# Hybrid RWKV-7 / sparse-attention step on one core: value products and turned pieces of the prompt attention in groups of four

## The chip, the cores and the metric

One Trainium2 chip, one of its cores. The time is that of the device in microseconds (us) for one execution of the whole kernel; several runs are shown, and the median is compared. The hardware profile is of one execution.

## What is computed

One layer of a hybrid decoder for a prompt of 1024 tokens and for 8 sampled tokens. After a projection, the kernel computes a recurrent branch (RWKV-7) and an attention branch with three parts: over compressed keys (63 of them), over selected blocks (for the prompt all earlier ones, since there are no more than 16 blocks of 64), and over a window of 512. Only the prompt's attention matters here. For each of 8 query tiles of 128 tokens, 8 heads in 2 groups, and 3 branches:

```python
s_s = jnp.einsum('btgjd,btgnld->btgjnl', qg, k_g) - slopes * s_dist
p_s = masked_softmax(s_s, s_dist >= 0)
o_s = jnp.einsum('btgjm,btgmd->btgjd', p_s, v_g)
...
o = g[:, :, 0] * o_c + g[:, :, 1] * o_s + g[:, :, 2] * o_w
```

All is float32. The sums of the three branches are added up in one place, since the gates and the reciprocal row sums are multiplied into the probabilities before the value products.

## The kernel before

The prompt attention is `attend_prompt` (L1759), one stage of the kernel between barriers. Its work is cut into 32 units n (4 heads of each group, j = n // 8, by 8 query tiles in the order 0, 4, 7, 1, 6, 2, 5, 3). The two groups g of a unit go together, as two matmuls for each block of keys. A unit goes through these steps:

- S, scores (L1817, TensorE): a step is up to 512 key columns, two groups, into PSUM banks 0 to 3; steps alternate between two bank pairs, and a step waits until the masks of the step two before are done. There are 88 steps.
- masks (L1911, VectorE): adds the distance term, writes the scores to SBUF and takes their extreme.
- exponentials (L1870, ScalarE), with row sums. They are held back and issued at the next even score step, for the two steps before it.
- row sums to reciprocals (L1919, L1921, VectorE), then the scaling with gates (L1965, GpSimd), 6 instructions for a unit.
- T, turned pieces (L1830, TensorE): a piece is two key blocks of 128, transposed for both groups, that is 4 transposes, into one PSUM bank: bank 4 for even pieces, bank 5 for odd ones. Before it, TensorE waits for the scaling and for the copy of the piece two before, which frees the bank.
- copies of turned pieces to SBUF (`probsT`, 5 slots): even pieces by ScalarE (L1886), odd ones by VectorE (L1942). A copy waits for its piece and for the value products that free its slot.
- V, value products (L1844, TensorE): for a piece 4 matmuls, recorded as 8 instructions, accumulated in bank 6 or 7 by the parity of the unit. Before them TensorE waits for the piece's copy, and at a unit's first piece for the closing product of the unit two before.
- closing product (L1927, VectorE), once per unit, after its last value products.

`PromptPlan` (L1636) writes the order out by hand, as one list of events that TensorE, ScalarE and VectorE all walk; each takes its own part of an event (VectorE does masks at S, odd copies at T, the closing product at V). GpSimd goes through the units by itself, SyncE only issues stores and weights. For every two score steps, `turns` adds the pieces: the value products of the pieces that were turned in the round before (`waiting`), and the next up to four turned pieces (`now`, five if more than 8 queue up). So a round is S S, then the pieces. At the end of the stage, rounds marked R have no scores. There are 160 pieces. Full rounds read S S V V T T V V T T; some have fewer of one or the other. `turns` stands at L1701 to L1708.

Of the kernel before, what the change touches and what calls it, by code (L numbers as in the profile page):

```python
# [1635 lines left out]
class PromptPlan:  # L1636
# [64 lines left out]
    def turns(self, s, queue, waiting, ready):  # L1701
        while ready < self.N and self.last_step[ready] + AT_LEAD <= s:
            queue = queue + list(range(self.first_of[ready], self.last_piece[ready] + 1))
            ready += 1
        now = queue[:AT_GROUP + (len(queue) > 8)]
        for a in range(0, max(len(waiting), len(now)), 2):
            self.events += [("V", pc) for pc in waiting[a:a + 2]] + [("T", pc) for pc in now[a:a + 2]]
        return queue[len(now):], now, ready  # L1708

    def by_need(self, n):  # L1710
# [1921 lines left out]
```

## Time and profile before

| | us |
|---|---|
| median of 3 runs | 1786.95 |
| lowest and highest | 1781.71, 1788.53 |
| profiled execution, its own time | 1775.88 |
| its span (first to last instruction) | 1774.1 |
| prompt attention in it | 754.1 to 999.2 |
| its three passes of the same shape | 59.50, 59.86, 59.49 |
| TensorE busy in the span | 1690.9 (95%) |
| VectorE, ScalarE, GpSimd busy | 814.6, 577.2, 376.7 |
| mean granted TensorE clock | 0.983 of full speed |

The profile names engines PE (TensorE matmul), PEld (TensorE weight load, which overlaps PE), DVE (VectorE), ACT (ScalarE), POOL (GpSimd) and SP (SyncE). In a timeline a row is several like instructions in a row, with the start, the time from the first start to the last end, and in brackets the idle time of the engine before it and who ended it. "issue" is idle time for which the profile shows no wait. Weight loads show the rhythm of TensorE best, since the ends of matmuls are modelled. A turned piece has 4 weight loads, a value piece 8.

### The profile page before, as it was taken

The numbers are of one execution on the slowest core, as the hardware profiler recorded it, in microseconds if no ns is written. First come the engines' busy times: TensorE is split into PE (matmuls) and PEld (weight loads), VectorE is DVE, ScalarE is ACT, GpSimd is POOL, SyncE is SP. The second block draws the span as 40 slices with busy tenths as digits, with TensorE's granted clock in tenths as the row PEclk, the third lists the DMA queues.
The fourth block names the chain that finished last, engine by engine and source line by source line (L and its number), as shares of the span: only waits on it lengthen the run. The fifth ranks groups of instructions, "written<-read, shape, count | busy, mean of one in ns | idle before, by whom it ended". The sixth has DMA issues, their size and how long they took to land. (4 is left out here: it accounts for less than half of the span.)

```text
span 1774.1 us, 40928 instructions
## 1 busy us (share of the span) xinstructions
PE 1690.9 (95%) x17848; PEld 1157.7 (65%) x17848; DVE 814.6 (46%) x1684; ACT 577.2 (33%) x1229; POOL 376.7 (21%) x442
## 2 busy tenths in 40 slices
PE   7999889999999989999999899899999999899997
PEld 5666566666666645667666689776568888545443
DVE  3100165455545419077666666272133356633444
ACT  4111245344343211276666221113322221111444
POOL 0211233232212100055655322103300013100110
PEclk9999899999999999999999899899999999999999
DMA  4112001000100045091200497529720141510001
GB/s 159 48 36 54 2 3 27 14 15 15 26 15 15 15 125 74 1 251 49 96 2 1 125 306 285 173 77 214 189 52 24 48 142 25 220 42 1 24 24 48
DMA packets 115463, 135.88 MB, mean 77 GB/s; under 512 B 48252, under 2 KB 97093, under 8 KB 110334
## 3 DMA queue, kind: packets, MB, share of 16 engines
q1 hardware_dynamic: 106034, 83.97, 17.2%
q0 software_dynamic: 9216, 49.29, 9.0%
q8 instruction: 142, 2.33, 0.6%
q14 instruction: 35, 0.29, 0.1%
q10 hardware_dynamic: 36, 0.01, 0.0%
HBM read 120.64 MB, written 16.62 MB: 77 GB/s over the span
## 5 line engine op out<-in xcount | busy, mean ns | idle before, releaser
L845 PE MATMUL ps<-xnT,rw_side_w 128*128 128x344 f32 x576 | 204.0, 479 | 0.0
L566 PE MATMUL ps<-xnT,w_z 128*128 128x344 f32 x624 | 182.0, 453 | 2.3 <-DVE xnT L654 1.3
L566 PEld LDWEIGHTS ps<-xnT,w_z 128*128 128x128 f32 x624 | 117.9, 190 | 62.9 <-issue 1.5
L1965 POOL TENSOR_SCALAR probs<-probs,row_sums,gates 128x63 f32<-128x63 f32 (+6 forms) x148 | 95.6, 662 | 229.8 <-DVE row_sums L1921 229.3
L845 PEld LDWEIGHTS ps<-xnT,rw_side_w 128*128 128x128 f32 x576 | 99.2, 191 | 40.3 <-issue 3.3
L2232 PE MATMUL ps<-xnT,zT 128*128 128x344 f32 x384 | 120.8, 463 | 0.0
L2232 PEld LDWEIGHTS ps<-xnT,zT 128*128 128x128 f32 x384 | 71.7, 194 | 36.0 <-issue 5.6
L278 PE MATMUL ps<-w_kv,xnT 128*128 128x396 f32 x256 | 89.6, 509 | 3.5 <-DMA w_kv<-in_w_in_dram 3.4
L1870 ACT ACTIVATE probs<-probs,neg_max 128x63 f32<-128x63 f32 (+6 forms) x148 | 87.5, 595 | 1.5 <-DVE neg_max L1911 1.5
L1817 PE MATMUL ps<-kT,zT 64*128 64x512 f32 (+3 forms) x384 | 73.7, 496 | 2.6 <-PEq L82 1.4
L278 PEld LDWEIGHTS ps<-w_kv,xnT 128*128 128x128 f32 x256 | 48.8, 194 | 40.7 <-DMA w_kv<-in_w_in_dram 7.8
L1844 PE MATMUL ps<-probsT,kvtok 128*64 128x128 f32 x1056 | 75.3, 280 | 0.0
L682 DVE SCALAR_TENSOR_TENSOR zT<-z_diff,vec,zT 128x1032 f32<-128x1032 f32 x13 | 16.8, 1294 | 126.2 <-POOL z_diff L540 113.5
L1830 PE MATMUL ps<-ident,probs 128*128 128x128 f32 (+1 forms) x460 | 68.1, 280 | 5.1 <-DVE probsT L1942 3.4
L1886 ACT ACTIVATE probsT<-ps 128x512 f32<-128x512 f32 (+1 forms) x80 | 45.9, 574 | 82.6 <-PE ps L1830 82.6
L1844 PEld LDWEIGHTS ps<-probsT,kvtok 128*64 128x64 f32 x1056 | 56.0, 136 | 24.0 <-issue 23.0
L2936 POOL TENSOR_TENSOR mT<-mT,gate_n 128x258 f32<-128x258 f32 x28 | 23.7, 854 | 218.0 <-DVE gate_n L2899 218.0
L1344 POOL TENSOR_TENSOR rw_Lb<-rw_Lm,level_mask 128x512 f32<-128x512 f32 x40 | 53.9, 1355 | 63.8 <-DVE rw_Lm L1513 38.8
L1942 DVE COPY probsT<-ps 128x512 f32<-128x512 f32 (+1 forms) x80 | 50.5, 632 | 36.0 <-PE ps L1830 35.1
L2835 ACT ACTIVATE zT<-ps 128x258 f32<-128x258 f32 x72 | 27.8, 387 | 109.0 <-PE ps L2819 86.2
L1830 PEld LDWEIGHTS ps<-ident,probs 128*128 128x128 f32 (+1 forms) x460 | 49.8, 140 | 17.9 <-issue 10.5
L628 ACT ACTIVATE zT<-ps 128x344 f32<-128x344 f32 x39 | 17.3, 464 | 132.7 <-PE ps L566 132.7
(560 smaller groups left out, 3263.7 us busy)
## 6 DMA issues: line engine op xcount, KB each, us to landing
w_z<-in_w_in_dram SPq DMA_DIRECT2D x13, 512.0 KB, 3.8
xnT_kept<-xnT SPq DMA_DIRECT2D x1, 4128.0 KB
x_tok<-in_x_prompt_dram SPq DMA_DIRECT2D x8, 512.0 KB
rw_side_w<-in_w_in_dram SPq DMA_DIRECT2D x16, 256.0 KB, 3.3
zT<-in_w_in_dram SPq DMA_DIRECT2D x8, 512.0 KB, 5.3
ring_k<-in_w_in_dram SPq DMA_DIRECT2D x8, 512.0 KB, 5.3
w_out<-in_w_out_dram SPq DMA_DIRECT2D x1, 4096.0 KB
h_tok<-in_x_prompt_dram SPq DMA_DIRECT2D x8, 512.0 KB, 8.4
```

The costliest lines, as they stand in the source:

```text
L278: last = nc.tensor.matmul(k.ps[:, u % 4, 0:half], k.xnT[:, c, i * P:(i + 1) * P], w[:, c, h * half:(h + 1) * half], start=(c == 0), stop=( ...
L566: last = nc.tensor.matmul(k.ps[:, u % 6, 0:CG], w[:, n % w_ring, c, :], k.xnT[:, c, g * CG:(g + 1) * CG], start=(c == 0), stop=(c == KC - 1))
L845: ins = nc.tensor.matmul(k.ps[:, SIDE_BANKS[g % 2], 0:CG], w.side[:, t % 2, c, :], k.xnT[:, c, g % 3 * CG:(g % 3 + 1) * CG], start=(c == 0 ...
L1344: nc.gpsimd.tensor_tensor(w.Lb[:, n % 2], w.Lm[:].rearrange("p q c n -> p (q c) n"), bc(k.tab["level_mask"][:, n + 1, :], 1, 8), ALU.mult) ...
L1817: last = nc.tensor.matmul(k.ps[:, 2 * (s % 2) + g, at:at + w], k.qT[half(g), j, i * P:(i + 1) * P], keys[half(g), t0:t0 + w], start=True, ...
L1830: last = nc.tensor.transpose(k.ps[0:m, 4 + pc % 2, (2 * b + g) * P:(2 * b + g + 1) * P], region(n, br, g, t * P, m), k.ident[:])
L1844: last = nc.tensor.matmul(k.ps[half(g), 6 + n % 2, 0:P], vals, pt[0:m, pc % NPT, (2 * b + g) * P:(2 * b + g + 1) * P], start=(br == 1 and ...
L1870: nc.scalar.activation(every, every, ACT.Exp, scale=-1.0, bias=neg_m[:, at:at + 1], accum_out=ls[:, at:at + 1]).then_inc(expd, 1)
L1886: nc.scalar.activation(to, src, ACT.Copy).then_inc(pt_a, 1)
L1942: nc.vector.tensor_copy(to, src).then_inc(pt_v, 1)
L1965: nc.gpsimd.tensor_scalar(every, every, ls[:, at:at + 1], k.gates[:, i, gate:gate + 1], ALU.mult, ALU.mult).then_inc(scaled, 1)
L2232: ins = self.nc.tensor.matmul(self.k.ps[:, self.banks[n % nb], 0:CG], self.w[:, t % 2, c, :], self.k.xnT[:, c, g * CG:(g + 1) * CG], start ...
```

## The change

In each round all value products come first, then all turned pieces, where before they came two and two in turn. Nothing else in the list changes, neither which pieces a round has nor where the exponentials stand. A full round reads S S V V V V T T T T.

```diff
--- before.py
+++ after.py
@@ -1703,8 +1703,7 @@
             queue = queue + list(range(self.first_of[ready], self.last_piece[ready] + 1))
             ready += 1
         now = queue[:AT_GROUP + (len(queue) > 8)]
-        for a in range(0, max(len(waiting), len(now)), 2):
-            self.events += [("V", pc) for pc in waiting[a:a + 2]] + [("T", pc) for pc in now[a:a + 2]]
+        self.events += [("V", pc) for pc in waiting] + [("T", pc) for pc in now]
         return queue[len(now):], now, ready
```

## Rows read from the trace of the kernel before

**Rows 1.** The page, busy time of each engine.
```profile
PE 1690.9 (95%) x17848; PEld 1157.7 (65%) x17848; DVE 814.6 (46%) x1684; ACT 577.2 (33%) x1229; POOL 376.7 (21%) x442
```

**Rows 2.** Stretches, two passes: length, busy us (instructions) by engine, clock, DMA.
```profile
780.84:840.34 59.50, 58.09 (x574) 41.06 (x572) 41.78 (x175) 39.53 (x116) 31.01 (x49) 1.00 0.29 104
840.34:900.20 59.86, 58.09 (x574) 41.06 (x572) 41.69 (x175) 39.51 (x116) 34.96 (x52) 1.00 0.19 72
```

**Rows 3.** Waits in the prompt attention: total us, times, longest.
```profile
ACT probsT L1886 <- PE ps L1830: 82.6, 70, 3.2
...
PEld ps L1844 <- issue: 27.9, 93, 0.8
...
PEld ps L1830 <- POOL probs L1965: 11.7, 26, 1.5
...
PE ps L1830 <- DVE probsT L1942: 5.1, 12, 1.3
```

**Rows 4.** Timeline, weight loads of one full round: start, us, engine, instructions.
```profile
780.84 0.85 PEld L1844 LDWEIGHTS ps<-probsT,kvtok 128*64 128x64 f32 x16 [0.76 <-issue]
781.86 0.86 PEld L1830 LDWEIGHTS ps<-ident,probs 128*128 128x128 f32 x8 [0.17 <-issue]
782.89 0.85 PEld L1844 LDWEIGHTS ps<-probsT,kvtok 128*64 128x64 f32 x16 [0.17 <-issue]
783.91 0.41 PEld L1830 LDWEIGHTS ps<-ident,probs 128*128 128x128 f32 x4 [0.17 <-issue]
...
784.94 0.30 PEld L1817 LDWEIGHTS ps<-kT,zT 64*128 64x128 f32 x4 [0.17 <-issue]
```

**Rows 5.** Timeline of the same round, copies of turned pieces.
```profile
782.56 0.60 ACT L1886 ACTIVATE probsT<-ps 128x512 f32<-128x512 f32 x1 [3.17 <-PE ps L1830]
783.00 0.69 DVE L1942 COPY probsT<-ps 128x512 f32<-128x512 f32 x1
```

**Rows 6.** Timeline, weight loads of the last rounds.
```profile
997.24 1.29 PEld L1844 LDWEIGHTS ps<-probsT,kvtok 128*64 128x64 f32 x24 [0.17 <-issue]
```

**Rows 7.** Timeline of a round with two value and four turned pieces.
```profile
776.03 0.86 PEld L1830 LDWEIGHTS ps<-ident,probs 128*128 128x128 f32 x8 [0.17 <-issue]
...
776.73 0.60 ACT L1886 ACTIVATE probsT<-ps 128x512 f32<-128x512 f32 x1 [0.80 <-PE ps L1830]
...
777.44 0.42 PEld L1830 LDWEIGHTS ps<-ident,probs 128*128 128x128 f32 x4 [0.55 <-POOL probs L1965]
...
777.54 0.68 DVE L1942 COPY probsT<-ps 128x512 f32<-128x512 f32 x1
...
778.34 0.42 PEld L1830 LDWEIGHTS ps<-ident,probs 128*128 128x128 f32 x4 [0.47 <-POOL probs L1965]
```

**Rows 8.** Stretches, rounds, each to the next scores; columns as in rows 2.
```profile
776.04:778.92 2.88, 2.27 (x18) 1.69 (x16) 2.15 (x14) 1.38 (x4) 2.88 (x6) 1.00 1.23 159
...
786.65:789.80 3.15, 3.15 (x40) 2.30 (x38) 2.56 (x14) 3.15 (x9) 0.40 (x1) 1.00 0.63 205
797.47:801.34 3.87, 3.87 (x48) 3.19 (x47) 2.61 (x9) 1.34 (x5) 0.10 (x1) 1.00 0.48 204
802.56:805.92 3.36, 3.36 (x40) 2.51 (x38) 2.74 (x12) 2.34 (x7) 1.68 (x2) 1.00 0.43 180
807.41:811.24 3.83, 3.48 (x38) 2.76 (x37) 3.18 (x25) 1.68 (x7) 2.91 (x6) 1.00 0.01 1
813.15:817.67 4.52, 4.14 (x50) 3.41 (x48) 3.35 (x12) 2.25 (x11) 2.81 (x7) 1.00 0.01 4
819.59:823.73 4.14, 4.06 (x48) 3.17 (x46) 3.37 (x11) 2.63 (x7) 1.58 (x2) 1.00 0.00 0
```

**Rows 9.** Stretches at the end of the stage, columns as in rows 2.
```profile
984.78:990.58 5.80, 4.10 (x41) 3.18 (x41) 1.85 (x5) 3.53 (x11) 5.45 (x9) 1.00 0.00 0
990.58:995.16 4.58, 4.58 (x57) 3.90 (x58) 1.76 (x3) 1.19 (x2) 1.12 (x3) 1.00 0.00 0
995.16:999.02 3.86, 3.86 (x54) 2.88 (x50) 1.03 (x3) 0.60 (x1) 0.00 (x0) 1.00 0.02 4
```

## The prediction, made before the change was run

> **What bounds the kernel now.** I read the page first, then the stretch that the change touches, then single rounds of it. The page says that TensorE is busy for 95% of the span [rows 1]. The prompt attention runs from 754.1 to 999.2 us (the table ahead), and in a whole pass of it TensorE is busy for 58.09 of 59.50 us at a granted clock of 1.00 [rows 2], which is its upper level of 2.4 GHz. So the order of its own work decides, and every wait that is put into its queue is paid in full unless one beside it goes. The waits say what the other engines do there: ScalarE, before its copies of turned pieces, sat idle 82.6 us for TensorE; TensorE waited for VectorE's copies only 5.1 us in 12 places [rows 3]. The copiers have time to spare, but a sum says nothing on how fast one copy answers.
>
> One round then shows the pattern [rows 4]: weight loads of two value pieces (16 loads, 0.85 us), a gap of 0.17, two turned pieces (0.86), a gap of 0.17, again two and two, and the next scores. The gap stands at each change of kind, whatever the semaphores do: the profile calls it "issue". The copies of the same round [rows 5] begin 0.70 us after the first turned piece's load (781.86 to 782.56, ScalarE, 0.60 long) and 1.14 us after it for the second piece (783.00, VectorE, 0.69 long). There are two PSUM banks for turned pieces, so the third piece waits for the first one's copy, the fourth for the second one's. In this round the third is loaded at 783.91, 0.75 us after the first copy ended at 783.16: the two value pieces between cover that answer entirely.
>
> **What the change does, step by step.** It permutes the events of a round; TensorE, ScalarE and VectorE all walk the same list, so nothing is added or removed, no DMA moves, and SyncE's and GpSimd's queues don't read the list. By the plan in the code 45 rounds have pieces (160 pieces in all), in four passes over the same eight query tiles, one for each pair of heads; I take a pass from one full round to the next like it, 59.50 us [rows 2].
>
> Step 1, what it saves. Changes of kind between value and turned pieces go from 117 to 48 in the list. Three value pieces in a row are there at the end of the stage: 24 loads in 1.29 us and no gap inside [rows 6]. So four take 1.72 + 0.17 = 1.89 us where two pairs take 2 x 1.02 = 2.04. Two changes fewer in a full round are worth 0.30 us, if nothing waits.
>
> Step 2, what it costs. The four turned pieces now stand together, with nothing between the second and the third. This too is in the trace, in the round of two value and four turned pieces that both orders share [rows 7]: loads at 776.03, ScalarE's copy from 776.73 for 0.60, the third piece at 777.44, that is 1.41 us after the first, 0.11 behind the end of the copy. (The row names GpSimd as releaser of this gap; the ScalarE copy ends at 777.33, just ahead of the load, and I take it for the releaser.) Without the wait it would follow at about 0.86 + 0.06. The second piece's copy is VectorE's: 1.14 + 0.69 + 0.12 = 1.95 us after the first load the fourth can start, and 0.58 later come the scores (778.34 to 778.92, the end of the first stretch of rows 8). So the block takes 1.95 + 0.58 = 2.53 us, where two pairs take 2 x 1.03 = 2.06. If VectorE has the first piece of the block, the third starts at 0.70 + 0.69 + 0.11 = 1.50, the fourth at 1.97, and the block takes 2.55.
>
> A full clean round is then 1.89 + 2.53 = 4.42 us after its scores, against 4.10 now [rows 4, 8]: 0.32 more. In the shared round of rows 7 the fourth piece came later still (2.31), because VectorE was at its masks and row sums when the second piece was ready. In the new order the turned pieces start a microsecond later behind the scores and VectorE is through: in rows 5 it comes to its copy straight from other work, 2.16 us after the first value piece (780.84 to 783.00), and the new order wants it there at 1.89 + 1.14 = 3.03. So I take 1.95, not 2.31; the 2.31 is the upper bound.
>
> Step 3, the other rounds of a pass, by the same pitches [rows 8]. In order of time, now and then: 4.10 to 4.42; 3.15 to 3.02 (only two turned pieces, a change of kind saved, no wait); the shared round stays; 3.87 to 4.41 (a small third piece covers less); 3.36 to 3.75; 3.83 to 4.15; 4.52 to 4.55; 4.14 to 4.48; and three more of these shapes, read in the same view, +0.37, +0.26 and +0.35. The 4.52 round gains almost nothing in length because it already has the wait (TensorE is busy for 4.14 of it): VectorE's copy came late behind masks, and in the new order it ends at the same moment. In the 3.83 round the closing product of a tile (L1927, 0.28 us), which VectorE now does before its copy and not behind it, adds 0.2 to a copy that TensorE waits for. The sum is +2.8 us per pass (0.32 - 0.13 + 0 + 0.54 + 0.39 + 0.32 + 0.03 + 0.34 + 0.98). The pattern stands three times; in the second pass, which is 59.86 us long, the extra 0.36 is such a late copy in the 4.14 round, which then adds nothing. So 3 x 2.79 - 0.34 = 8.0; the next four rounds, of the first four kinds, give 0.7, one round near the start -0.1.
>
> Step 4, the end of the stage, where there are no scores and five turned pieces may stand in a row [rows 9]. The last round with scores is of the 3.36 kind; what follows it starts 0.36 later. In the next stretch of 5.80 us TensorE is busy for only 4.10: it waits for copies that stand behind row sums and exponentials; the exponentials stand behind a copy that is 0.36 later, and VectorE's copy gets the product of 0.28 in front of it: +0.3. Then 4.58 to 4.84, and the last stretch, whose last value pieces wait for the last turned pieces' copies without two value pieces as cover, 3.86 to 4.29. Together 0.36 + 0.3 + 0.26 + 0.43 = +1.3 us.
>
> The other queues: score steps wait for the masks of two steps before. By rows 5 VectorE is through with the masks 2.16 us into a round and the next scores come 4.10 us into it, so a longer round only gives more room. GpSimd's scaling is waited for in 26 places, 11.7 us together [rows 3]; most of them are the 0.17 gap under another name, and pieces that start later wait less: between -2 and 0, I take 0. The value pieces' own wait is on copies of the round before, which end while the next scores run. Behind the stage comes a barrier, and the next stage starts with it: nothing catches the delay up.
>
> The sum: 8.0 + 0.7 - 0.1 + 1.3 = **+9.9 us**. The profiled execution took 1775.88 us, 1.8 more than its span of 1774.1 and 11 less than the median of 1786.95 (the table ahead); the same steps stand in either, so I add the same 9.9: 1785.8 for an execution like the profiled one, 1796.9 for the median.
>
> One rule on the clock bears on this. In the shared round four turned pieces took 2.88 us and the granted clock was 1.00 throughout [rows 8], the upper level; TensorE was busy for 2.27 of it. The Trainium skill, page "TensorE: Matmul & The Clock Gate", section "Part 4: PE-mode transpose", says that transposes do not count as activity for the clock in the way matmuls do, which speaks against grouping them. By it the fourth rival below would hold; the trace's own group of four does not agree.
>
> **The rivals.** First, the other side: the third piece doesn't wait. If a copy answered within the 0.92 us that two turned pieces last, only step 1 would be left, some 69 changes of kind at 0.15 = -10 us: 1777. The point is 1.41 us against 0.92, and rows 7 measure 1.41; the ScalarE copy alone is 0.60. Chance 0.03.
>
> Second, the wait is hidden in most rounds as in the 4.52 one: if VectorE's and ScalarE's copies come late already, the old order pays the same. Then only some rounds add, half of the sum: +4 to +6, 1792. For it speak the 5.1 us that TensorE waits for VectorE now [rows 3]; against it, that TensorE is idle in few rounds (none in 3.87 of 3.87 and 3.36 of 3.36 [rows 8]). Chance 0.17.
>
> Third, the block is as long as in rows 7, 2.89 us and not 2.53, because a copier is late there too: 0.36 more in about 25 rounds, +9: +19, 1806. Against it stands the later start behind masks. Chance 0.13.
>
> Fourth, the clock falls to its lower level of 1.2 GHz in the groups: their 1.7 us of loads and more double in some 40 rounds, +70 us, 1865. Rows 8 speak against it. Chance 0.01.
>
> My forecast has 0.66, with an own range of 1793 to 1801: between the bounds of the waits (about 2 us either way) and the spread of medians.
>
> **How the numbers follow.** The likeliest case gives 1796.9. The runs shown spread from 1781.71 to 1788.53, so a median of a few moves by 2 to 3 us. The range reaches down into the second rival and up to the edge of the third: 1789 to 1805. About 0.5%, or 8.9 us, is what a measurement of this kernel can tell from no change, and +9.9 lies just over it. Of the forecast's 0.66 I give 0.40 to slower by over 0.5% and 0.26 to within; the third and fourth give 0.14 to slower, the second 0.02 to slower and 0.15 to within, the first 0.03 to faster. That is slower 0.56, within 0.41, faster 0.03.
>
> **What would show it.** In the profile after, a full round should have 32 value loads in one row of 1.7 us, one gap of 0.17, 8 loads of turned pieces, then an idle of about 0.5 us put down to ScalarE's or VectorE's copy, and some 4.4 us to the next scores; TensorE's wait for ScalarE's copies, hardly there now, should come near 10 us, and "issue" at the value pieces from 27.9 us down by some 5 to 7. TensorE's busy time should hardly change. If the third piece comes under 1.2 us after the first, step 2 is wrong; if the fourth comes at 2.3, the third rival holds; if the stage grows by under 7 us with these waits seen, the pitches of step 1 are too small; if anything behind 999.2 us moves other than by the shift, the carry through the barrier is wrong.

## The result and the profile after

The changed kernel is slower: 1793.45 us (20 runs, 1782.84 to 1801.44) against 1780.68 (20 runs, 1771.2 to 1788.53), a ratio of 1.0069 with a 95% interval of 1.0048 to 1.0091. In a second comparison on another occasion (the first experiment below) the ratio was 1.0029, 0.9997 to 1.0062. One of the ten runs of after in it took 1985.83 us at a granted clock of 0.841, where the others had 0.981 to 0.984, and is left out of the ratio. Both intervals hold what the traces of the attention say: it grew by 10.0 us, 0.56% of the whole. The median of before over more runs is 6 us lower than that of the first three, on which the forecast's absolute time was built.

| us | before | after |
|---|---|---|
| profiled execution, its own time | 1775.88 | 1797.99 |
| span | 1774.1 | 1796.1 |
| prompt attention, first score matmul to last value matmul | 244.74 | 254.76 |
| the rest of the span | 1529.4 | 1541.3 |
| TensorE busy in the span | 1690.9 | 1694.9 |
| granted clock | 0.983 | 0.981 |

The profiled execution of after is 22 us longer, and 12 of these lie outside the attention; a section below says what they are. All lines of the changed function stand one lower in the profile of after (L1829 for L1830).

A clean round is one in which TensorE waits for nobody in before. The full clean round that [rows 4] and [rows 5] show for before, in the timeline of after (start, us, engine, instructions, idle before and its end):

```profile
782.73 1.73 PEld L1843 LDWEIGHTS ps<-probsT,kvtok 128*64 128x64 f32 x32 [0.76 <-issue]
784.63 0.85 PEld L1829 LDWEIGHTS ps<-ident,probs 128*128 128x128 f32 x8 [0.17 <-issue]
785.32 0.60 ACT L1885 ACTIVATE probsT<-ps 128x512 f32<-128x512 f32 x1 [4.08 <-PE ps L1829]
785.76 0.69 DVE L1941 COPY probsT<-ps 128x512 f32<-128x512 f32 x1 [0.99 <-PE ps L1829]
786.03 0.41 PEld L1829 LDWEIGHTS ps<-ident,probs 128*128 128x128 f32 x4 [0.55 <-issue]
786.06 0.63 PE L1829 MATMUL ps<-ident,probs 128*128 128x128 f32 x4 [0.34 <-ACT probsT L1885]
786.56 0.42 PEld L1829 LDWEIGHTS ps<-ident,kT 128*128 128x128 f32 x4
...
787.15 0.30 PEld L1816 LDWEIGHTS ps<-kT,zT 64*128 64x128 f32 x4 [0.17 <-issue]
```

Four value pieces in one row of 32 loads, 1.73 us, and one gap of 0.17: 1.90 from the first of them to the first turned piece. The third turned piece comes 1.40 us after the first (784.63 to 786.03), 0.11 behind the end of ScalarE's copy; the row of the weight loads calls this idle time "issue", the matmul row of the same moment names the copy. The fourth comes 1.93 after the first, 0.11 behind VectorE's copy. The scores follow at 4.42.

Stretches of after: the three passes [rows 2], then rounds of the first, in order, that answer to [rows 4] and [rows 8] (length, busy us and instructions of PE, PEld, DVE, ACT, POOL, granted clock, DMA):

```profile
782.74:845.09 62.35, 58.12 (x576) 41.08 (x574) 42.15 (x175) 39.75 (x116) 30.98 (x49) 1.00 0.28 102
845.09:907.69 62.60, 58.11 (x576) 41.07 (x574) 42.39 (x174) 39.74 (x116) 34.94 (x52) 1.00 0.18 69
907.69:969.99 62.30, 58.13 (x576) 41.10 (x574) 42.19 (x175) 39.74 (x116) 30.90 (x48) 1.00 0.01 2
...
782.73:787.15 4.42, 4.08 (x50) 3.41 (x48) 2.73 (x9) 1.02 (x2) 0.09 (x1) 1.00 1.12 337
788.87:791.87 3.00, 3.00 (x41) 2.31 (x39) 2.23 (x13) 2.23 (x7) 0.35 (x1) 1.00 0.61 203
799.60:804.02 4.42, 3.95 (x50) 3.19 (x48) 2.58 (x7) 1.62 (x5) 0.08 (x1) 1.00 0.56 238
805.24:808.99 3.75, 3.41 (x42) 2.51 (x40) 2.69 (x12) 2.12 (x7) 2.09 (x3) 1.00 0.67 283
810.47:814.48 4.01, 3.48 (x40) 2.76 (x38) 3.16 (x25) 1.66 (x7) 2.70 (x6) 1.00 0.00 1
816.40:820.92 4.52, 3.98 (x52) 3.43 (x50) 3.35 (x11) 2.23 (x11) 2.60 (x7) 1.00 0.02 4
822.84:827.46 4.62, 4.18 (x50) 3.14 (x48) 3.53 (x11) 2.61 (x7) 2.08 (x3) 1.00 0.00 0
```

Passes are 2.85, 2.74 and 2.81 us longer than the 59.50, 59.86 and 59.49 of before, TensorE's busy time in them is the same (58.12 against 58.09), and the clock is at its upper level. The waits, against [rows 3] (total us, times, longest):

```profile
PEld ps L1843 <- issue: 24.4, 72, 0.8
...
PEld ps L1829 <- issue: 20.2, 68, 1.0
PEld ps L1829 <- POOL probs L1964: 11.7, 22, 0.9
PEld ps L1829 <- POOL kT L1964: 6.1, 8, 1.6
PE ps L1829 <- DVE probsT L1941: 5.6, 14, 0.8
...
PE ps L1829 <- ACT probsT L1885: 4.9, 14, 0.5
```

The same two kinds of row in before, which [rows 3] does not show:

```profile
PEld ps L1830 <- issue: 13.2, 62, 0.7
...
PE ps L1830 <- ACT probsT L1886: 0.3, 1, 0.3
```

TensorE waits for ScalarE's copies 14 times, where before it did once (0.3 us). This view alone would mislead: the same wait stands here under "issue", under ScalarE and, where a scaling came about as late, under GpSimd. The rounds' lengths are what adds up.

### The profile page after: what moved, and what is told of

Its sections match the earlier page's. It is cut to its first block and busy times, and to the rows that moved or that the text cites. A ratio compares the mean times of both kernels' runs of the same rounds, so it can differ in the third digit from the quotient of the medians.

```text
span 1796.1 us, 40928 instructions
## 1 busy us (share of the span) xinstructions
PE 1694.9 (94%) x17848; PEld 1159.7 (65%) x17848; DVE 814.8 (45%) x1684; ACT 578.0 (32%) x1229; POOL 376.7 (21%) x442
## 5 line engine op out<-in xcount | busy, mean ns | idle before, releaser
L1829 PE MATMUL ps<-ident,probs 128*128 128x128 f32 (+1 forms) x460 | 69.4, 279 | 14.1 <-ACT probsT L1885 4.6
L1843 PE MATMUL ps<-probsT,kvtok 128*64 128x128 f32 x1056 | 70.9, 278 | 0.5 <-ACT probsT L1885 0.5
L1829 PEld LDWEIGHTS ps<-ident,probs 128*128 128x128 f32 (+1 forms) x460 | 49.6, 140 | 29.3 <-issue 17.2
```

The lines of the kernel that those rows point to most:

```text
L1829: last = nc.tensor.transpose(k.ps[0:m, 4 + pc % 2, (2 * b + g) * P:(2 * b + g + 1) * P], region(n, br, g, t * P, m), k.ident[:])
L1843: last = nc.tensor.matmul(k.ps[half(g), 6 + n % 2, 0:P], vals, pt[0:m, pc % NPT, (2 * b + g) * P:(2 * b + g + 1) * P], start=(br == 1 and ...
```

## The experiments

All lengths of "the attention" run from the first score matmul to the last value matmul, 244.74 in before and 254.76 in after. Three comparisons below rest on 10 or more runs of each kernel and give a ratio (the changed kernel again, and the two orders with turned pieces on both sides); every other experiment is one profiled execution, and only its trace is read.

**The changed kernel again.** No edit.

> The changed kernel once more, unchanged. Theory (the order of the attention alone costs time, what lies behind it only shifts): the prompt attention is again 10.0 us longer than the 245.1 us of before, to 0.3 us, and the 8 to 9 us that TensorE waits in the compression of the sampled caches in the first profile of after (at its first use of the value weights cmp_w1v) come and go from one execution to the next, in the kernel before as well. Rival (the later start makes these weights collide with the gathers): the wait of 8 to 9 us is there again, and it belongs to the change.

```profile
756.08:1011.40 255.32, 235.48 (x2287) 165.88 (x2288) 168.70 (x687) 160.27 (x465) 127.06 (x196) 0.99 0.23 70
```

The attention took 255.3 us, 10.6 more than before: a little over the 0.3 us I had allowed. The stretch from the first score matmul to the first turned piece, which is the same in both orders, is where the two profiles of after differ (before, after, after again):

```profile
754.13:763.27 9.14, 7.88 (x40) 4.23 (x40) 6.62 (x37) 7.62 (x25) 2.37 (x6) 0.74 0.96 403
...
756.58:765.15 8.57, 7.41 (x40) 4.04 (x40) 6.62 (x37) 7.62 (x25) 2.36 (x6) 0.79 1.01 426
...
756.08:765.27 9.19, 8.49 (x40) 4.37 (x40) 6.62 (x37) 7.62 (x25) 2.36 (x6) 0.68 0.96 401
```

Its 40 matmuls take 8.57 to 9.19 us, the shorter the higher the granted clock (0.79, 0.74, 0.68 of full speed). From the first turned piece on, the attention took 235.60 us in before, 246.19 in after and 246.13 in after again: the change costs 10.6 and 10.5, and the 10.0 of the first profile holds 0.6 us of a faster start. The wait in the compression stage was not there; the 12 us outside the attention in the first profile of after shrink to 3 (1787.7 - 255.3 = 1532.4). The ratio here is 1.0029 (0.9997 to 1.0062).

**Copies slowed in both orders.** Ahead of each copy of a turned piece its engine copies 256 columns to a place that nobody reads (the diff is cut: a semaphore wait of each engine on its own earlier extra copy and the two buffers are left out here):

```diff
+                    nc.scalar.activation(aside[0][0:m, :], src[:, 0:256], ACT.Copy).then_inc(twice_a, 1)
                     nc.scalar.activation(to, src, ACT.Copy).then_inc(pt_a, 1)
...
+                    nc.vector.tensor_copy(aside[1][0:m, :], src[:, 0:256]).then_inc(twice_v, 1)
                     nc.vector.tensor_copy(to, src).then_inc(pt_v, 1)
```

In the order of before:

> The order of before, but ahead of each copy of a turned piece its engine copies 256 columns of it to a place that nobody reads, 0.38 us on ScalarE and 0.42 on VectorE. Theory: in the full clean round the copy has 0.64 us to spare, so its 4.10 us stay; only rounds in which the third or fourth piece waits already get longer, by about 0.4 each, which are some 20: the attention is 6 to 10 us longer than 245.1. Rival (the copiers' total load decides, not the single answer): the order does not matter, and the attention grows as much as in the order of after.

In the order of after:

> The order of after with the same extra copies. Theory: nothing covers the copy between the second and the third turned piece, so every round with three or more of them grows by 0.4: the full clean round from 4.42 to 4.84 us, and the attention by 14 to 18 us over the 254.8 of after. Rival: it grows by as much as in the order of before, 6 to 10 us.

Timeline of the full clean round with slowed copies in the order of after:

```profile
783.08 0.85 PEld L1831 LDWEIGHTS ps<-ident,probs 128*128 128x128 f32 x8 [0.17 <-issue]
...
783.78 0.38 ACT L1890 ACTIVATE aside_a<-ps 128x256 f32<-128x256 f32 x1 [3.66 <-PE ps L1831]
784.06 0.59 ACT L1891 ACTIVATE probsT<-ps 128x512 f32<-128x512 f32 x1
...
784.76 0.41 PEld L1831 LDWEIGHTS ps<-ident,probs 128*128 128x128 f32 x4 [0.83 <-issue]
```

Stretches, order of before and then order of after: the full clean round, and the attention.

```profile
787.02:791.12 4.10, 4.10 (x51) 3.42 (x49) 3.06 (x10) 1.21 (x4) 0.00 (x0) 1.00 1.08 316
...
759.77:1017.87 258.10, 238.97 (x2287) 167.93 (x2288) 193.66 (x767) 181.19 (x545) 127.66 (x196) 0.97 0.23 69
```

```profile
781.19:785.94 4.75, 4.13 (x50) 3.41 (x49) 3.05 (x10) 1.36 (x4) 0.00 (x0) 1.00 1.10 328
...
754.45:1023.84 269.39, 235.98 (x2288) 166.61 (x2288) 193.87 (x767) 181.61 (x545) 127.69 (x196) 0.99 0.22 66
```

The clean round is the test: 4.10 as before in one order, 4.75 instead of 4.42 in the other. The engines start the real copy 0.28 us after the extra one (783.78 to 784.06), not 0.38, so the answer is 0.28 to 0.34 slower and the third piece follows it: 1.68 us after the first instead of 1.40. The round of before has that much to spare, the round of after has none. The totals, +13.4 and +14.6 us, lie closer together than I expected: 6 to 10 was too little for the order of before. Its late rounds grew by 0.6 us (4.52 to 5.13), one of them by 0.95 (4.50 to 5.45); I take VectorE's extra work on top of late masks for the reason. Its rounds without scores at the end grew by 3.5 us, and most of that is the clock:

```profile
1004.54 0.92 PEld L1832 LDWEIGHTS ps<-ident,probs 128*128 128x128 f32 x8 [2.06 <-POOL kT L1975]
...
1006.00:1010.00 4.00, 3.59 (x23) 2.96 (x24) 1.28 (x3) 0.77 (x2) 1.40 (x3) 0.50 0.00 0
```

After 2.06 us without a weight load the granted clock fell from 1.00 to 0.50, its lower level of 1.2 GHz (1.00 up to 1004 us, 0.82 in the next two, 0.50 from 1006 to 1012). In these last rounds (996.87 to 1017.87) TensorE was busy for 18.61 us, against 15.75 in before for the same work, so by estimate 2.9 of the 13.4 us are the clock's. In the order of after it fell there too, after 2.22 us idle (17.28 busy against 15.86: 1.4 of the 14.6). Without it the two are 10.5 and 13.2, a little over and a little under what I had expected. A mean over the whole stage would not have told the two theories apart.

**A third bank for turned pieces.** All value sums go to bank 6, every third turned piece to bank 7; so that nothing reads bank 6 while it is written, the closing product leaves the value sums out.

```diff
-                if pc >= 2:
-                    pe.wait_ge(pt_v if pc % 2 else pt_a, (pc - 2) // 2 + 1)
+                if pc >= 3:
+                    pe.wait_ge(pt_a if pc % 2 else pt_v, (pc - 3) // 2 + 1)
...
-                nc.vector.tensor_tensor(dst, k.ps[:, 6 + n % 2, 0:P], dst, ALU.mult).then_inc(gatedo, 1)
+                nc.vector.tensor_tensor(dst, dst, dst, ALU.mult).then_inc(gatedo, 1)
```

> The order of before, with a third PSUM bank for turned pieces: all value sums go to bank 6, and bank 7 takes every third turned piece. The closing product leaves out the value sums (it squares its other operand), so that nothing reads bank 6 while TensorE writes it. Theory (only the answer of the copy two pieces back makes turned pieces wait): rounds without a wait keep their length (the full clean one 4.10 us); those that had one lose it, some 2 to 5 us in all; the attention takes 240 to 243 us instead of 245.1. Rival (the wait has another source, scaling or the copiers' load): no change.

> The order of after with the same third bank and the same part left out. Theory: the third turned piece no longer waits, and two changes of kind less are all that is left of the change, so the full clean round takes 3.80 us (4.42 in after, 4.10 in before), and the attention is 8 to 10 us shorter than with three banks in the order of before: 231 to 235 us. The sign of the change turns round. Rival (four turned pieces in a row are slow by themselves, whatever the banks): the round stays over 4.2 us and the attention over 245 us.

Stretches, order of before, then order of after: the full clean round, the late round of 4.52, the attention.

```profile
778.87:782.96 4.09, 4.09 (x50) 3.41 (x48) 2.73 (x9) 0.92 (x2) 1.12 (x3) 1.00 1.09 323
...
809.93:814.03 4.10, 4.10 (x51) 3.41 (x49) 3.35 (x12) 2.25 (x11) 3.22 (x8) 1.00 0.02 4
753.35:989.09 235.74, 232.51 (x2287) 165.68 (x2288) 169.12 (x687) 159.58 (x465) 129.87 (x196) 0.99 0.25 75
```

```profile
780.74:784.62 3.88, 3.88 (x50) 3.43 (x48) 2.73 (x9) 1.02 (x2) 1.17 (x3) 1.00 1.10 327
...
811.46:815.54 4.08, 3.99 (x51) 3.44 (x49) 3.63 (x12) 2.24 (x11) 3.05 (x8) 1.00 0.02 4
755.35:989.51 234.16, 228.09 (x2288) 166.30 (x2288) 168.47 (x687) 160.53 (x465) 128.72 (x196) 0.99 0.25 76
```

With the bank's wait gone the change turns its sign, as the theory wants: 234.2 against 235.7 us, and the clean round 3.88 against 4.09. But it gains 1.6 us, not 8 to 10. The timeline says why: three turned pieces now stand in one row of loads, and the fourth waits for the copy of the first in its turn (784.04, 0.11 behind 783.33 and 0.60):

```profile
782.63 1.29 PEld L1829 LDWEIGHTS ps<-ident,probs 128*128 128x128 f32 x12 [0.17 <-issue]
783.33 0.60 ACT L1885 ACTIVATE probsT<-ps 128x512 f32<-128x512 f32 x1 [3.79 <-PE ps L1829]
...
784.04 0.42 PEld L1829 LDWEIGHTS ps<-ident,kT 128*128 128x128 f32 x4
```

The wait is short in the clean round (0.07 us), but some 0.4 where VectorE has to copy the first one or is late (such a round takes 4.29 us, against 4.02 in the order of before), and 0.9 in one round of the second pass. In the order of before the third bank is worth 9.0 us: late rounds (4.52) shrink to 4.10 and the shared rounds lose both their waits. I had expected 2 to 5; I had counted only TensorE's waits that the profile puts down to VectorE.

**Can the third bank be had?** The same with the closing product whole; the first value piece of a unit then waits for the closing product of the one before.

> The order of before with the third bank for turned pieces and the whole computation: the closing product reads bank 6 again, and so the first value piece of a unit waits until the closing product of the unit before is done. Theory: the third bank gives back what the run without the value sums in the closing product showed (235.7 us of attention instead of 244.7), but 31 unit boundaries now wait for VectorE, which is at its masks for the first 2 us of a round: 0.4 to 1.5 us each where no turned piece stands between, so the attention takes 245 to 260 us. Rival (VectorE answers in the shadow of other pieces): it stays under 241 us, and the third bank is worth having.

> The same with the order T T V V V V T T. The first value piece then stands a microsecond later behind the scores, nearer to the end of the masks. Theory: boundaries at the start of a group wait less, those inside it as much: 0 to 5 us shorter than in the order of before with the same waits.

```profile
PEld ps L1844 <- DVE zT L1927: 17.9, 18, 2.2
PE ps L1844 <- DVE zT L1927: 13.6, 18, 2.0
```

The attention took 251.9 and 253.5 us. This view of the first of them has 18 waits of TensorE for the closing product, 17.9 us together: more than the 9 that the bank gives. The longest, 2.20 us, was again followed by a fall of the granted clock (1.00 up to 900 us, 0.62 in the next two us and 0.53 in the two behind them), and its round took 6.92 us instead of 3.36. The split order made the attention 1.6 longer, not shorter, so there my expectation was wrong. I take the reason to be that its value pieces stand in one block, and a unit's end in the middle of it has no turned piece behind which to wait; no run isolates that.

**One and one.** V T V T V T V T.

```diff
-        for a in range(0, max(len(waiting), len(now)), 2):
-            self.events += [("V", pc) for pc in waiting[a:a + 2]] + [("T", pc) for pc in now[a:a + 2]]
+        for a in range(max(len(waiting), len(now))):
+            self.events += [("V", pc) for pc in waiting[a:a + 1]] + [("T", pc) for pc in now[a:a + 1]]
```

> One value piece, one turned piece, in turn (V T V T V T V T). Theory: four more changes of kind in a full round than before, at 0.15 us each, and one piece between any two turned ones: by the loads the third piece comes 1.3 us behind the first one, just short of the 1.41 that the first copy takes. So a full round is 0.6 to 0.8 us longer than its 4.10, and the attention 15 to 25 us longer than before, 260 to 270 us. Rival (a change of kind costs nothing by itself, the gap is only how the profile shows it): the attention is within 5 us of before.

```profile
778.18 0.42 PEld L1844 LDWEIGHTS ps<-probsT,kvtok 128*64 128x64 f32 x8 [0.76 <-issue]
778.77 0.42 PEld L1830 LDWEIGHTS ps<-ident,probs 128*128 128x128 f32 x4 [0.17 <-issue]
779.35 0.42 PEld L1844 LDWEIGHTS ps<-probsT,kvtok 128*64 128x64 f32 x8 [0.17 <-issue]
```

The gap of 0.17 stands at every change, and the full clean round takes 4.70 us: four changes more, 0.60 us, 0.15 each. The attention took 260.1 us, 15.4 more than before. The whole list has 130 changes between value and turned pieces more, which at 0.15 would be 19.5; the rounds that waited in before grew less (3.83 stays 3.83), since each turned piece now has a value piece as cover. The third piece stood 2.35 us behind the first (778.77 to 781.12), not the 1.3 I had expected. A change of kind has a price of its own, without any wait.

**Turned pieces on both sides.** T T V V V V T T: four changes where before has five, and neither pair of turned pieces is next to the other, since scores follow the second one.

```diff
-        for a in range(0, max(len(waiting), len(now)), 2):
-            self.events += [("V", pc) for pc in waiting[a:a + 2]] + [("T", pc) for pc in now[a:a + 2]]
+        head = now[:2] if len(now) > 2 else []
+        self.events += [("T", pc) for pc in head] + [("V", pc) for pc in waiting] + [("T", pc) for pc in now[len(head):]]
```

> In each round two turned pieces stand ahead of all the value products and the rest behind them (T T V V V V T T). Theory (the third piece waits for the first one's copy unless other work lies between, and each change of kind costs some 0.15 us): four changes in a full round where before has five, the copies covered on both sides by value pieces or scores, so the attention is 2 to 4 us shorter than before, 241 to 243 us, and the kernel 0.1 to 0.2% faster than before. Rival (the turned pieces so close behind the scores meet VectorE at its masks, as in the shared rounds): the first copy by VectorE ends at about 2.8 us into the round, which is when the third piece wants its bank, so some rounds wait and the attention is as long as before or up to 3 us longer.

```profile
778.26:782.21 3.95, 3.95 (x51) 3.44 (x49) 2.63 (x9) 0.93 (x2) 0.00 (x0) 1.00 1.13 338
...
751.19:993.67 242.48, 231.82 (x2287) 166.13 (x2288) 167.62 (x687) 158.69 (x465) 126.98 (x196) 0.99 0.25 73
```

The clean round takes 3.95 us, one change less than 4.10, and the attention 242.5, 2.3 less than before. The late round stays at 4.52. Over all runs the ratio is 1.0002 (0.9969 to 1.0035): 0.13% can't be seen in the time of the whole kernel, only in the trace. The rounds without scores at the end lost 0.8 us (18.30 against 17.45), so the last run took this order only where there are scores (the other branch, not shown, is the split order above):

```diff
+        if s >= len(self.steps):
+            for a in range(0, max(len(waiting), len(now)), 2):
+                self.events += [("V", pc) for pc in waiting[a:a + 2]] + [("T", pc) for pc in now[a:a + 2]]
+        else:
```

> T T V V V V T T in the rounds with scores, and the order of before in the rounds at the end that have none. Theory: the parts add up: the score rounds keep the 3.1 us that the split order saved there, and the end of the stage takes the 17.4 us of before and not the 18.3 of the split order. The attention takes 241.4 to 242.0 us instead of 244.7, by the profile; 0.17% of the whole, which the interval of the times will hardly show. Rival: the end takes longer because the last score round hands over its pieces in another order: 242.5.

The attention took 241.7 us, 3.0 less than before, and the parts add up. The ratio of the times is 1.0005 (0.9972 to 1.0038), which neither shows nor excludes a gain of 0.17%.

## Where the profiled time outside the attention went

The span less the attention, for each profile: before 1529.4, after 1541.3, after again 1532.4, split 1523.0, one and one 1526.5, three banks 1526.7 and 1530.5, slowed copies 1534.5 and 1538.3, three banks whole 1534.4 and 1541.8, split in score rounds 1540.2. It moves by 19 us. The kernels of all twelve profiles are the same outside the attention, so a single profiled execution can't show this change by its span, and intervals of the ratio are 0.2 to 0.35% either way. Two parts of the 19 us can be named. The attention begins anywhere from 751.0 to 759.8 us, which is 9 us of scatter ahead of anything that was changed. The other is a wait.

In the first profile of after it is one wait in the compression of the sampled caches, at the first use of the weights `cmp_w1v`:

```profile
PEld ps L2064 <- DVE xnT L2169: 8.7, 1, 8.7
...
PE ps L2064 <- DVE xnT L2169: 8.3, 1, 8.3
```

After it the granted clock fell to 0.50 here as well, and the 1024 matmuls with these weights took 65.5 us instead of the 63.9 of before: 8.3 + 1.6 are 10 of the 12 us. The same wait of 5 to 8 us stands in three more profiles: the slowed copies in the order of after, the third bank whole in the split order, and the split order in score rounds. These four have the four longest rests, 1538.3 to 1541.8; the other eight, before and the second profile of after among them, don't have it, and there the weights' matmuls took 63.9 us each time.

The 16 transfers that bring the weights are in SyncE's queue for 53.38 us in the first profile of after (the row below), 39.87 in before and 48.84 in the second profile of after:

```profile
1022.55 53.38 SPq L1984 DMA_DIRECT2D cmp_w1v<-in_cmp_w_dram  x16
```

The profile names VectorE's transposes as releaser. By the code TensorE waits here for five things: its own transposed input, the hidden values, the projection and the scores of an earlier unit, and the weights. By the timeline of after the first four were done by 1080 us and TensorE's work ahead of it by 1083.3, and the matmuls began at 1091.6, so the weights are what is left. That is argued and not tested: the queue's row ends at 1075.93 and does not show when the data had landed, and its length does not separate the profiles (47.67 us in one with the wait, 48.84 in one without). The wait came in four of the seven profiles in the order of after or a split order, and in none of the five others; that the change makes it likelier is not excluded, but the second profile of after shows that it does not bring it about each time.

## Why the prediction was right, point by point

The forecast was +9.9 us for the attention and 1796.9 for the median; measured were +10.0 in the trace (10.6 in the second) and 1793.45, inside the range of 1789 to 1805. Part of that closeness is luck. The absolute time was built on a median of before that was 6.3 us too high, and the medians lie 12.8 apart where 9.9 was forecast, which took some of it back. In the trace the 10.0 holds 0.6 us of a faster start; the change itself is 10.6, so the mechanism's sum was 0.7 too small.

- The bound: right. TensorE's busy time in a pass did not change, and every wait put into its queue appeared in the time. (The plan has 46 rounds with pieces, not 45; no sum uses the number.)
- Step 1, a change of kind at 0.15 us: right, shown by itself in one and one (0.60 for four) and in the split order (4.10 to 3.95).
- Step 2, the answer of a copy: right to 0.01 us. The third piece comes at 1.40 (1.41 was read from the shared round), the block takes 2.52, the round 4.42. That it is the bank's wait and not the grouping itself is shown by the third bank (3.88) and by the slowed copies (4.10 stays, 4.42 goes to 4.75).
- Step 3, the other rounds: forecast 3.02, 4.41, 3.75, 4.15, 4.55, 4.48; measured 3.00, 4.42, 3.75, 4.01, 4.52, 4.62. Two are off by 0.14, in opposite directions. At 4.15 the closing product ahead of VectorE's copy was priced at 0.2. In the timeline of after it begins at 812.48, before the first turned piece is ready for its copy, and the copy at 812.65, 0.80 after the load at 811.85 where 0.70 is the least: 0.1 of delay, and the third piece at 1.59 and not 1.70. At 4.48 I left out a gap: the compressed values (63 rows instead of 128) have their own 0.17 on both sides. The shared round, which I had kept, grew by 0.05 in this pass. The three passes gave 8.4 instead of 8.0.
- The rounds ahead of the first pass were given -0.1 and stayed as long (17.57 and 17.58 us). The 0.6 by which the stage began faster in the first profile of after stands ahead of the first turned piece and is not in the second profile. The four rounds behind the passes gave 0.8, forecast 0.7.
- Step 4, the end without scores: +1.4 (17.45 to 18.86), forecast +1.3. Together 8.4 + 0.8 + 1.4 = 10.6.
- The carry through the barrier: nothing gave the 10 us back, but the rest scatters by more than the change. "Only the shift" can be said of the second profile of after (from the end of the attention to the first use of `cmp_w1v` 71.0 us, against 72.2 in before), not of the first (80.3).
- The rivals. No wait (1777): falls with the 1.40. Hidden in most rounds: falls, since clean rounds are the rule, though the 4.52 round behaves so. A block as long as in the shared round: falls, the fourth piece comes at 1.93 and not 2.31. The clock: it was granted in full, 1.00, in the groups of four of after. The Trainium skill, page "TensorE: Matmul & The Clock Gate", section "Part 4: PE-mode transpose", would have transposes count less for the clock; in these groups, between value and score matmuls, no run here shows an effect. Where the clock did fall inside the attention (slowed copies, closing product), TensorE had sat idle for over 2 us just before.
- The signs named ahead came, but two were smaller than named. The wait for ScalarE's copies is 4.9 us in the view, not near 10, because most of it is listed under "issue" at the turned pieces' loads, which went from 13.2 us to 20.2. "Issue" at the value pieces fell by 3.5 us (27.9 to 24.4), less than the 5 to 7 I had named.

## What to carry to other kernels

A producer with two buffers needs other work between its second and its third piece, as long as the consumer's whole answer, not its busy time: here 1.41 us from the start of a piece to the reuse of its bank, of which the copy is 0.60. Grouping like work saves only the change of kind (0.15 us here), so group the work that waits for nothing, and lay it between the pairs that wait. Price such a change from rounds of the trace that already have the new order, and check it by the length of a round; the time of the whole kernel scattered here by more than the change.

## What the runs showed of the hardware

- TensorE's weight loads have a gap of 0.17 us at each change between these kinds of tile (128x64 value blocks, 128x128 transposes, 64-row scores), also between value blocks of 128 and 63 rows of one piece, where the code has no wait; it costs 0.15 us net (4.10, 4.70 and 3.95 us with five, nine and four changes).
- Two copies one after the other on ScalarE start 0.28 us apart where the first is 0.38 long; on VectorE a copy starts 0.17 after a product of 0.25. Rows overlap at their ends, so a sum of durations is too high by about 0.1 each.
- Sixteen weight transfers of 128 KB stood in SyncE's queue for 38.91 to 53.38 us in profiles of kernels with the same stage, and TensorE waited 5 to 8 us at their first use in four of twelve. What makes them slow in one execution is left open.
- A wait of TensorE can cost more than its length. After 2.06, 2.22, 2.20 and 8.7 us without a weight load (slowed copies in both orders, the third bank whole, after) the granted clock fell from 1.00 to some 0.50, and the work behind took 2.9, 1.4 and 1.6 us longer in the first, second and last of them. In the last rounds of before and after the longest such gap was 1.47 and 1.62 us, and the clock stayed at 1.00.
- At the start of the stage the same 40 matmuls took 8.57 to 9.24 us at granted clocks of 0.79 to 0.64.
